# Three 1024-wide parts of an input projection (v, u, gate a) as seven half-size products each, in a hybrid decoder block on one Trainium2 core

## The chip, the cores and the metric

The kernel runs on 1 core of one Trainium2 chip. The metric is the device time of one execution in microseconds (us). An execution under the hardware profiler gives, beside its own time, a trace of every engine: TensorE (PE), VectorE (DVE), ScalarE (ACT), GpSimd (POOL), SyncE (SP), and of the transfers.

## The reference, cut to what matters

512 tokens of 1024 features go through one decoder block in fp32. The change touches only the first projection:

```python
h = rms_norm(x, g_mix)                       # x * rstd(token) * g_mix(feature)
z = h @ w_in                                 # [512, 1024] @ [1024, ...]
u, v, q_lat, kv_lat, k_rope, gate_a, gate_b = split(z)   # 1024, 1024, 384, 256, 64, 1024, 1024 wide
y_a = spatial_gating(gelu(u), gelu(v), ...)  # layer norm over v's 1024 columns, then a mix in chunks of 128 tokens
y_b = mla_attention(q_lat, kv_lat, k_rope, ...)
x = x + (sigmoid(gate_a) * y_a + sigmoid(gate_b) * y_b) @ w_o
# then a mixture of experts and a gated embedding: not touched
```

## The kernel before

Every fp32 matrix is split for TensorE into a high part (rounded to the type fp32r) and a low part (the rest). A product is three matmuls for each block of 128 features (a k-block): high rows by high weights, low rows by high weights, high rows by low weights. ScalarE makes the high part (a copy with rounding), VectorE the low part (the weights less their high part).

The projection runs in ten column chunks w = 0 to 9, in this order: q's latent (384 wide), the kv latent with the rope key (320 wide), v in two halves of 512, u in two, gate a in two, gate b in two. `z_chunk` does one chunk: 4 token tiles of 128 rows by 8 k-blocks by 3 matmuls, 96 in all (L1789, L1790, L1793), each token tile in one of four PSUM banks. SyncE's queue loads the weights of a chunk in one transfer (2048 KB for 512 columns) into one of the two buffers `win`; `split(w)` of ScalarE (L787) writes the high part times g_mix, `split(w)` of VectorE (L1222, one instruction with two inputs in SBUF for each k-block) the low part. The rows are x transposed, without g_mix. `evac` of ScalarE (L821 to L837) takes a finished bank out, for gate a in the bank itself, where VectorE multiplies it into u (L1299). `evac(1, t)` (L825, L826, L828) has three activations for one token tile: the kv latent, its sum of squares, that of the rope key. After chunk 9 attention goes on with transposes (L1743). GpSimd makes constants at the start, turns q by the rope tables (L627 to L629) and gathers rows for the experts later.

Each engine works through its own program in the order in which it is written; waits on semaphores stand in front of the instruction that needs them. So the order of the functions' calls for each engine decides what stands behind a wait.

## Time and profile before

| | us |
|---|---|
| runs | 1111.62, 1109.51, 1111.4 (median 1111.4) |
| the profiled execution's own time | 1110.49 |
| its span in the trace | 1108.7 |
| busy in the span: PE, PEld | 1092.9, 914.7 |
| busy in the span: DVE, ACT, POOL | 861.2, 787.0, 423.6 |

The span goes from the first to the last instruction in the trace; the execution's own time is 1.8 us more. PE is the matmuls, PEld the loads of the 128x128 operand that stays in the array, which run beside matmuls. Busy times of engines lie beside each other, so only the one that is waited for sets the end.

### The profile page before, as it was taken

What the parts mean: (1) busy time and instruction counts of PE and PEld (TensorE: products, weight loads), DVE (VectorE), ACT (ScalarE), POOL (GpSimd) and SP (SyncE); (2) the same over time, 40 slices, a digit from 0 to 9 for tenths busy, and PEclk for the clock granted to TensorE, in tenths of its full rate; (3) what the DMA queues carried; (4) which work ended last, traced back from release to release, by engine and by line L of the source; (5) the groups of instructions that cost most, each with busy time, mean ns of one, the idle gap of its engine ahead of it and who ended that gap; (6) DMA issues with size and microseconds to landing.
All of it is one profiled execution on the core that took longest, in us unless ns stands there. A gap on an engine that the chain in (4) does not pass through costs nothing.

```text
span 1108.7 us, 17836 instructions
## 1 busy us (share of the span) xinstructions
PE 1092.9 (99%) x5488; PEld 914.7 (83%) x5488; DVE 861.2 (78%) x1239; ACT 787.0 (71%) x1270; POOL 423.6 (38%) x477
## 2 busy tenths in 40 slices
PE   7999999999999999999999999999999999999998
PEld 7988888878778888888888888888888888888787
DVE  4535532278765468999999999999999999999865
ACT  6644433357654343888888898889888988888772
POOL 1120000015276003355556555555655555555400
PEclk9999999999999999999999999999999999999999
DMA  7422422112402259999999999999999999999632
GB/s 251 153 76 76 142 85 76 29 57 71 158 1 71 101 225 381 356 377 382 394 393 388 391 393 388 391 391 393 395 396 396 396 394 393 392 393 359 192 151 76
DMA packets 72130, 291.60 MB, mean 263 GB/s; under 512 B 15187, under 2 KB 20598, under 8 KB 47126
## 3 DMA queue, kind: packets, MB, share of 16 engines
q1 hardware_dynamic: 52672, 254.13, 57.3%
q0 software_dynamic: 18768, 34.79, 12.5%
q10 hardware_dynamic: 646, 2.12, 0.5%
q8 instruction: 24, 0.39, 0.1%
q14 instruction: 20, 0.16, 0.0%
HBM read 284.61 MB, written 42.07 MB: 295 GB/s over the span
## 4 chain that ended last, share of the span: by engine, by line
PE 93%; DVE 3%; ACT 2%; POOL 1%; issue 1%; DMA 0%; ACTq 0%; POOLq 0%; DVEq 0%
PE bank L2065 11%; PE bank L2067 11%; PE bank L2066 11%; PE bank L1752 7%; PE bank L1789 6%; PE bank L1793 6%; PE bank L1790 6%; PE bank L2093 5%; PE bank L2091 5%; PE bank L2092 5%; PE bank L2030 5%; PE bank L1743 2%; PE bank L1944 1%; PE bank L2163 1%; PE bank L2165 1%; PE bank L2164 1%
## 5 line engine op out<-in xcount | busy, mean ns | idle before, releaser
L1624 DVE TENSOR_TENSOR arena_r<-arena,win_r 128x1024 fp32r<-128x1024 f32 x252 | 292.0, 1221 | 21.9 <-ACT win_r L1082 19.1
L1082 ACT ACTIVATE win_r<-arena 128x1024 fp32r<-128x1024 f32 x252 | 246.5, 1069 | 0.5 <-DMA resid<-in_w_exp_up 0.5
L2065 PE MATMUL bank<-win_r,work_r 128*128 128x512 f32 x512 | 206.5, 403 | 0.6 <-issue 0.6
L2066 PE MATMUL bank<-win_r,x_low_r 128*128 128x512 f32 x512 | 199.5, 390 | 0.0
L2067 PE MATMUL bank<-arena_r,work_r 128*128 128x512 f32 x504 | 197.4, 392 | 0.0
L1604 DVE TENSOR_TENSOR arena_r<-arena,hT_r 128x1024 fp32r<-128x1024 f32 x128 | 150.5, 1217 | 0.5 <-ACT hT_r L1090 0.5
L733 POOL DMA_INDIRECT moe_sum<-ya,sidx x64 | 111.5, 1743 | 102.7 <-ACT ya L1118 86.0
L1789 PE MATMUL bank<-arena_r,hT_r 128*128 128x512 f32 (+2 forms) x320 | 121.9, 381 | 2.2 <-DVE win_r L1222 2.1
L1790 PE MATMUL bank<-arena_r 128*128 128x512 f32 (+2 forms) x320 | 121.1, 378 | 0.0
L1793 PE MATMUL bank<-win_r,hT_r 128*128 128x512 f32 (+2 forms) x320 | 121.0, 378 | 0.0
L2067 PEld LDWEIGHTS bank<-arena_r,work_r 128*128 128x128 f32 x504 | 94.6, 188 | 21.7
L2065 PEld LDWEIGHTS bank<-win_r,work_r 128*128 128x128 f32 x512 | 96.7, 189 | 18.8 <-issue 0.7
L2066 PEld LDWEIGHTS bank<-win_r,x_low_r 128*128 128x128 f32 x512 | 96.4, 188 | 18.6
L2091 PE MATMUL bank<-hT_r,work_r 128*128 128x512 f32 x256 | 105.2, 411 | 0.0
L708 POOL COPY small<-ya 128x1 f32 (+1 forms) x64 | 104.1, 1627 | 1.1 <-DMA ya<-h_rows,gidx 1.1
L2093 PE MATMUL bank<-arena_r,work_r 128*128 128x512 f32 x256 | 100.5, 393 | 0.0
L2092 PE MATMUL bank<-hT_r,work_r 128*128 128x512 f32 x256 | 100.0, 391 | 0.0
L1222 DVE SCALAR_TENSOR_TENSOR win_r<-win,small,arena_r 128x512 fp32r<-128x512 f32 (+2 forms) x80 | 54.2, 748 | 57.0 <-ACT arena_r L787 57.0
L693 POOL DMA_INDIRECT ya<-h_rows,gidx x66 | 69.7, 1055 | 53.1 <-POOL gidx L690 51.9
L627 POOL TENSOR_TENSOR work<-arena 128x256 f32<-128x256 f32 x10 | 7.7, 770 | 197.0 <-DVE arena L1378 180.9
L1589 DVE TENSOR_TENSOR x_low_r<-bank,work_r 128x512 fp32r<-128x512 f32 x128 | 82.0, 682 | 0.3 <-ACT work_r L1055 0.2
L1055 ACT ACTIVATE work_r<-bank 128x512 fp32r<-128x512 f32 x128 | 69.5, 595 | 13.3 <-PE bank L2030 11.5
(321 smaller groups left out, 2213.4 us busy)
## 6 DMA issues: line engine op xcount, KB each, us to landing
arena<-in_w_exp_down SPq DMA_DIRECT2D x64, 1024.0 KB
arena<-in_w_exp_gate SPq DMA_DIRECT2D x63, 1024.0 KB
arena<-in_w_exp_up SPq DMA_DIRECT2D x63, 1024.0 KB
win<-in_w_in SPq DMA_DIRECT2D x8, 2048.0 KB, 7.8
win<-in_w_o SPq DMA_DIRECT2D x2, 2048.0 KB, 7.9
arena<-in_w_ple_gate SPq DMA_DIRECT2D x2, 2048.0 KB, 13.7
arena<-moe_sum SPq DMA_DIRECT2D x7, 512.0 KB, 7.0
win<-in_mla_w_qb SPq DMA_DIRECT2D x4, 576.0 KB, 4.0
```

Of the source, the lines that this page charges most:

```text
L1082: act.activation(gu_hi[n % 2][:, :, cols], raw[:, :, cols], ACT.Copy).then_inc(gu_hi_r, 1)
L1604: dve.tensor_tensor(wdn_lo[j % RING][:, k, :], wdn[j % RING][:, k, :], wdn_hi[j % 2][:, k, :].bitcast(F32), ALU.subtract).then_inc(dn_lo, 1)
L1624: dve.tensor_tensor(low_[:, :, cols], raw[:, :, cols], gu_hi[n % 2][:, :, cols].bitcast(F32), ALU.subtract).then_inc(gu_lo_r, 1)
L1789: pe.matmul(b_, x_hi, w_hi, start=(k == 0), stop=False)
L1790: last = pe.matmul(b_, x_lo, w_hi, start=False, stop=False)
L1793: last = pe.matmul(b_, x_hi, w_lo, start=False, stop=(k == KD - 1))
L2065: pe.matmul(b_, x_hi[:, k, :], w_hi, start=(k == 0), stop=False)
L2066: pe.matmul(b_, x_lo[:, k, :], w_hi, start=False, stop=False)
L2067: last = pe.matmul(b_, x_hi[:, k, :], low_[:, :, k * FF:(k + 1) * FF], start=False, stop=(k == KD - 1))
L2091: pe.matmul(b_, hi, w_hi, start=(k == 0), stop=False)
L2092: pe.matmul(b_, lo, w_hi, start=False, stop=False)
L2093: last = pe.matmul(b_, hi, wdn_lo[n % RING][:, k, cols], start=False, stop=(k == KF - 1))
```

## The change

v, u and gate a (p = 0, 1, 2 in the new code) are cut in 2 x 2 blocks, tokens by columns, and their 1024 features in two halves. Eight products of half size become seven (Strassen's scheme in Winograd's form) at the price of sums ahead of and behind the products. They run in the order 11, T1, T2, 21, 22, T3, T4, each of 2 token tiles (i = 0, 1) by 4 k-blocks by 3 matmuls = 24 matmuls of 512 columns (L2243 to L2245), with banks by pairs. q's latent, the kv latent and gate b stay as they were.

- **Rows.** g_mix is now on the rows (when x is transposed: four activations of 128x128 for each half in `hT_evac`, L925; the low part multiplies by g_mix too, L1443). The weights are copied as they are, and VectorE's low part is a plain subtraction (L1547). Four sums of rows S1 to S4 (128x1024 each) are made by VectorE once (`rows_1` to `rows_4`, L1457 to L1479) and split like weights (`high_part`, `low_part`).
- **Weights.** Each half-size block has 128x2048 elements and is worked on in two parts of 128x1024. GpSimd makes the sums T1, T2 and T3 (`add_weights`, L749: for v T1, T2, T3; for u and for gate a T1, T3, T2), VectorE T4 (`last_weights`, L1504). ScalarE makes the high part of each block (L1009; L1002 for S), VectorE the low part (L1495; L1488 for S). They come in transfers of 1 MB where a chunk had one of 2 MB.
- **Outputs.** `add_products` (VectorE, L1520 to L1538) takes the products out of PSUM and adds them, two instructions of 128x512 for each of X, Y, 11, 12, 22, W, 21, each with one input in PSUM. "11" goes out first by ScalarE (`first_product_out`, L1014). `gelu` (L1022, L1024) works in SBUF.
- **Order.** evac(1, t) stands between the high parts of v in ScalarE's order; TensorE's product 11 of v waits for evac(1, i) to free its banks. v's layer-norm statistics for tokens 0 to 255 (`v_stats` 0 and 1) stand behind u's last sum, those for 256 to 511 between gate a's sums 12 and 22, and the split of chunk 8 (`FIRST`) between W and 21.
- **Buffers.** `resid` serves as a weight buffer, so x's rows are loaded again after T4 of gate a.

VectorE's order behind the low part of chunk 1. Before, that low part (L1222, 128x320) is followed by the rope angles and, behind them, the low parts of the 512-wide chunks:

```order
L1222 SCALAR_TENSOR_TENSOR win_r<-win,small,arena_r 128x320 x8
L1250 TENSOR_TENSOR work<-small,inv_freq 128x128
L1252 TENSOR_SCALAR work<-work 128x128
L1253 TENSOR_SCALAR work<-work 128x128
L1254 SCALAR_TENSOR_TENSOR work<-work 128x128
```

Now it is followed by the sums of rows and the low parts of v; `arena` holds S1, S2 and high parts, `work` S4, `rope_q` S3, `hT_r` is the high part of the rows, `resid`, `ya` and `win` hold weights (L1457 and L1458 are the two short pieces of one sum):

```order
L1463 TENSOR_TENSOR arena<-hT_r 128x1024
L1457 TENSOR_TENSOR arena<-arena,arena_r 128x512
L1458 TENSOR_TENSOR arena<-arena,arena_r 128x512
L1465 TENSOR_TENSOR arena<-arena,arena_r 128x1024
L1495 TENSOR_TENSOR arena_r<-resid,arena_r 128x1024 x2
L1495 TENSOR_TENSOR ya_r<-ya,arena_r 128x1024 x2
L1469 TENSOR_TENSOR arena<-arena,arena_r 128x1024
L1470 TENSOR_TENSOR arena<-arena,hT_r 128x1024
L1488 TENSOR_TENSOR arena_r<-arena,arena_r 128x1024
L1479 TENSOR_TENSOR work<-arena,hT_r 128x1024
L1457 TENSOR_TENSOR work<-work,arena_r 128x512
L1458 TENSOR_TENSOR work<-work,arena_r 128x512
```

The angles now stand behind v's last sum. GpSimd's order behind its constants, before (`gqr` is a gain, then the rope constants):

```order
L601 AFFINE_SELECT arena<-arena 128x1024
L605 TENSOR_SCALAR gqr<-gqr 128x64
L610 TENSOR_TENSOR arena<-work,gqr 128x128 x4
L610 TENSOR_TENSOR arena<-work,gkr 128x128 x4
L614 IOTA small 128x4
```

and now, where the 18 sums of weights stand in between (rows 2 to 4: T1, T2, T3 of v; then T1, T3, T2 of u and of gate a):

```order
L749 TENSOR_TENSOR resid<-ya 128x1024 x2
L749 TENSOR_TENSOR resid<-resid,win 128x1024 x2
L749 TENSOR_TENSOR ya<-ya,win 128x1024 x2
L749 TENSOR_TENSOR resid<-resid,win 128x1024 x2
L749 TENSOR_TENSOR win<-win 128x1024 x2
L749 TENSOR_TENSOR resid<-resid,win 128x1024 x4
L749 TENSOR_TENSOR win<-win 128x1024 x2
L749 TENSOR_TENSOR resid<-resid,win 128x1024 x2
L755 TENSOR_SCALAR gqr<-gqr 128x64
```

ScalarE's order at the start of v, now (`resid` is T1, `ya` block 11; L1002 are S1, S2 and S4; L986 to L989 are evac(1, t)). Before, this place had evac(1, 0) to evac(1, 3) with the next chunk's eight 128x512 copies of L787 between them:

```order
L1009 ACTIVATE arena_r<-resid 128x1024 x2
L1009 ACTIVATE arena_r<-ya 128x1024 x2
L1002 ACTIVATE arena_r<-arena 128x1024
L986 ACTIVATE arena<-bank,small 128x320
L987 ACTIVATE work,small<-bank,small 128x256
L989 ACTIVATE work,small<-bank,small 128x64
L1002 ACTIVATE arena_r<-arena 128x1024
L986 ACTIVATE arena<-bank,small 128x320
L987 ACTIVATE work,small<-bank,small 128x256
L989 ACTIVATE work,small<-bank,small 128x64
L1002 ACTIVATE work_r<-work 128x1024
L1009 ACTIVATE arena_r<-resid 128x1024 x2
```

So evac(1, 1), for which TensorE's product 11 waits with its second token tile, now stands behind S2's high part, and that behind VectorE's `rows_2`.

The diff, cut to its core:

```diff
+        NP = 3
+        in_res0, in_res1 = in_res
+        B_RAW = [{"11": in_ya[0], "T1": in_res0, "T2": in_res0, "21": in_w0[1], "22": in_w0[0], "T3": in_ya[1], "T4": in_res0}]
+        B_RAW += [{"11": in_w0[1], "T1": in_res[p % 2], "T2": in_res[p % 2], "21": in_w0[0], "22": in_w1[1], "T3": in_w1[0],
+                   "T4": in_res[p % 2]} for p in range(1, NP)]
+        B_HI = [{"11": in_v[0], "T1": in_v[1], "T2": in_hi[0], "21": in_tab, "22": in_ln, "T3": in_hi[0], "T4": in_hi[1]}]
+        B_HI += [{"11": in_hi[0], "T1": in_tab, "T2": in_hi[1], "21": in_tab, "22": in_ln, "T3": in_hi[0],
+                  "T4": in_tab if p == NP - 1 else in_hi[1]} for p in range(1, NP)]
+        B_LO = [{**B_RAW[0], "T1": in_ln, "T2": in_hi[1]}] + [{**B_RAW[p], "T1": in_ln, "T2": in_hi[0]} for p in range(1, NP)]
...
+        PRODUCTS = ("11", "T1", "T2", "21", "22", "T3", "T4")
+        PRODUCT_ROW = {"T1": "S1", "T2": "S2", "22": "S4", "T3": "S3"}
+        PRODUCT_BANK = {"11": 0, "T1": 4, "T2": 2, "21": 6, "22": 0, "T3": 4, "T4": 6}
+        HIGHS = [("T1", "11", "S1", "S2", "S4", "T2", "21", "22", "S3", "T3", "T4")] + [("T1", "11", "T2", "21", "22", "T3", "T4")] * (NP - 1)
+        LOWS = [("T1", "11", "S1", "S2", "T2", "S4", "21", "22", "S3", "T3", "T4")] + [("T1", "11", "T2", "21", "22", "T3", "T4")] * (NP - 1)
...
+        WEIGHTS_ORDER = [(0, n) for n in ("T1", "T2", "T3")] + [(p, n) for p in range(1, NP) for n in ("T1", "T3", "T2")]
...
+            def pairs_loads():
+                sp.wait_ge(tr_done, 2 * NT)
+                sp.wait_ge(rms_sq, NT)
+                half_load(v2(xr_, 2 * D, HK, 512), half_chunk(1, BASE[1]), ld_w0[0], 32)
+                free(0)
+                half_load(v2(win0, 0, HK, 512), half_chunk(0, "22"), win_ready[0], 32)
...
+                for p in range(2, NP):
+                    sp.wait_ge(pj_done, products_done(p - 2, "T4"))
+                    half_load(v2(xr_, p % 2 * 2 * D, HK, 512), half_chunk(p, BASE[p]), ld_w0[0], 16 + 16 * p)
+                    sp.wait_ge(pj_done, products_done(p - 1, "11"))
...
+            def add_weights(p, name):
+                done = 2 * WEIGHTS_ORDER.index((p, name))
+                if done:
+                    pool.wait_ge(weights_added, done)
+                term = "22" if name != "T1" else "11" if BASE[p] == "12" else "12"
+                pool.wait_ge(*raw_landed(p, term))
+                if name == "T1" and p == 0:
+                    pool.wait_ge(*raw_landed(0, "11"))
+                    pool.wait_ge(tr_done, 2 * NT)
+                    pool.wait_ge(rms_sq, NT)
+                elif name == "T1":
+                    pool.wait_ge(ld_w0[0], 16 + 16 * p)
+                elif name == "T3":
+                    pool.wait_ge(*raw_landed(p, "12"))
+                else:
+                    pool.wait_ge(lo_ready, split_count(LOWS, p, "T1"))
+                for part in range(2):
+                    dst, other = B_RAW[p][name][part][0], (B_RAW[p]["T3"] if term == "12" else B_RAW[p][term])[part][0]
+                    src = B_RAW[0]["11"][part][0] if name == "T1" and p == 0 else dst
+                    pool.tensor_tensor(dst, src, other, ALU.add).then_inc(weights_added, 1)
+            for p, name in WEIGHTS_ORDER:
+                add_weights(p, name)
...
-                    act.activation(whi_r[:, k, 0:n], v2(win[w % 2], 0, KD, n)[:, k, :], ACT.Copy,
-                                   scale=gmix[:, k:k + 1]).then_inc(hi_ready, 1)
+                    if w == FIRST:
+                        act.wait_ge(pj_done, products_done(NP - 1, "T3" if k < HK else "T2"))
+                    elif w >= 1:
+                        act.wait_ge(whi_used, KD * (w - 1 if w == 1 else w - 1 - 2 * NP) + k + 2)
+                    z = slice(k, k + step)
+                    act.activation(whi_r[:, z, 0:n], v2(win[w % 2], 0, KD, n)[:, z, :], ACT.Copy).then_inc(hi_ready, step)
...
+            high_part(0, "T1")
+            high_part(0, "11")
+            high_part(0, "S1")
+            evac(1, 0)
+            high_part(0, "S2")
+            evac(1, 1)
+            high_part(0, "S4")
+            act.wait_ge(whi_used, 2 * KD)
+            high_part(0, "T2")
+            evac(1, 2)
+            evac(1, 3)
+            high_part(0, "21")
+            first_product_out(0)
+            high_part(0, "22", products_done(0, "T1"))
+            high_part(0, "S3")
+            high_part(0, "T3", products_done(0, "T2"))
+            high_part(0, "T4", products_done(0, "T2"))
+            for p in range(NP):
+                gelu(p, "11")
+                if p + 1 < NP:
+                    high_part(p + 1, "T1", products_done(p, "21"))
+                gelu(p, "12")
+                if p + 1 < NP:
+                    high_part(p + 1, "11", products_done(p, "T3"))
+                else:
+                    split(FIRST, range(HK))
+                    split(FIRST, range(HK, KD))
+                gelu(p, "22")
+                gelu(p, "21")
+                if p + 1 < NP:
+                    first_product_out(p + 1)
+                    high_part(p + 1, "T2", products_done(p, "T4"))
+                    high_part(p + 1, "21", products_done(p + 1, "T1"))
+                    high_part(p + 1, "22", products_done(p + 1, "T1"))
+                    high_part(p + 1, "T3", products_done(p + 1, "T2"))
+                    high_part(p + 1, "T4", products_done(p + 1, "21" if p + 1 == NP - 1 else "T2"))
...
-                    dve.scalar_tensor_tensor(v2(win_r[w % 2], 0, KD, n)[:, k, :], v2(win[w % 2], 0, KD, n)[:, k, :],
-                                             gmix[:, k:k + 1], whi_r[:, k, 0:n].bitcast(F32), ALU.mult, ALU.subtract).then_inc(lo_ready, 1)
...
+            def rows_1():
+                for i in range(2):
+                    dve.wait_ge(tr_free[i], NT)
+                link(dve.tensor_tensor(S1, row_hi(lower, second), row_hi(upper, second), ALU.subtract))
+                link(lower_lo(S1, second, ALU.add))
+                dve.tensor_tensor(S1, S1, row_lo(0, second), ALU.subtract).then_inc(combined, 1)
...
+            def rows_2():
+                dve.wait_ge(combined, 1)
+                link(dve.tensor_tensor(S2, S1, row_lo(0, first), ALU.add))
+                dve.tensor_tensor(S2, S2, row_hi(upper, first), ALU.add).then_inc(combined, 1)
...
+            def low_part(p, name, room=None):
+                if room is not None:
+                    dve.wait_ge(pj_done, room)
+                if name[0] == "S":
+                    dve.wait_ge(hi_ready, split_count(HIGHS, p, name))
+                    dve.tensor_tensor(s_lo[name], s_raw[name], s_hi[name].bitcast(F32), ALU.subtract).then_inc(lo_ready, 1)
+                    return
+                for part in range(2):
+                    dve.wait_ge(hi_ready, split_count(HIGHS, p, name, part))
+                    reader = {"11": "T1", "21": "T4", "22": "T2" if p else "T3"}.get(name)
+                    if reader is not None:
+                        dve.wait_ge(*added(p, reader, part))
+                    dve.tensor_tensor(B_LO[p][name][part][1], B_RAW[p][name][part][0], B_HI[p][name][part][1].bitcast(F32),
+                                      ALU.subtract).then_inc(lo_ready, 1)
+            def last_weights(p):
+                dve.wait_ge(*raw_landed(p, "21"))
+                dve.wait_ge(lo_ready, split_count(LOWS, p, "T2"))
+                for part in range(2):
+                    dst = B_RAW[p]["T4"][part][0]
+                    dve.tensor_tensor(dst, dst, B_RAW[p]["21"][part][0], ALU.add).then_inc(combined, 1)
...
+                product = {"X": "T2", "Y": "T1", "11": "21", "12": "22", "22": "T3", "W": "T3", "21": "T4"}[quad]
...
+                        dve.tensor_tensor(C21, b_, C12, ALU.subtract).then_inc(pj_free[2 + i], 2)
...
+            rows_1()
+            low_part(0, "T1")
+            low_part(0, "11")
+            rows_2()
+            low_part(0, "S1")
+            rows_4()
+            low_part(0, "S2")
+            low_part(0, "T2")
+            last_weights(0)
+            low_part(0, "S4")
+            low_part(0, "21")
+            low_part(0, "22")
+            rows_3()
+            low_part(0, "S3")
...
+            for p in range(NP):
+                add_products(p, "X")
+                add_products(p, "Y")
+                low_part(p, "T3")
+                low_part(p, "T4")
+                add_products(p, "11")
+                if p == 2:
+                    gated_quad("11")
+                if p + 1 < NP:
+                    low_part(p + 1, "T1", products_done(p, "22"))
+                add_products(p, "12")
+                if p == 2:
+                    gated_quad("12")
+                    v_stats(2)
+                    v_stats(3)
+                add_products(p, "22")
+                add_products(p, "W")
+                if p + 1 < NP:
+                    low_part(p + 1, "11")
+                else:
+                    split(FIRST, range(HK))
+                    split(FIRST, range(HK, KD))
+                add_products(p, "21")
+                if p == 0:
+                    means_and_angles()
+                elif p == 1 and NP == 3:
+                    v_stats(0)
+                    v_stats(1)
+                if p + 1 < NP:
+                    low_part(p + 1, "T2", products_done(p + 1, "11"))
+                    last_weights(p + 1)
+                    low_part(p + 1, "21")
+                    low_part(p + 1, "22")
...
+                    for k in range(HK):
+                        if i == 0 and k % 2 == 0:
+                            pe.wait_ge(lo_ready, split_count(LOWS, p, name, k // 2))
+                        if row is not None:
+                            a_hi, a_lo = s_hi[row][:, k, tok(i)], s_lo[row][:, k, tok(i)]
+                        else:
+                            k_, q = (k if name == "11" else k + HK), tok(i + 2 if name == "T4" else i)
+                            a_hi, a_lo = hT_hi[:, k_, q], lo_[k_][:, q]
+                        w_hi, w_lo = B_HI[p][name][k // 2][1][:, k % 2, :], B_LO[p][name][k // 2][1][:, k % 2, :]
+                        b_ = bank[b0 + i][:, :]
+                        pe.matmul(b_, a_hi, w_hi, start=(k == 0), stop=False)
+                        pe.matmul(b_, a_lo, w_hi, start=False, stop=False)
+                        last = pe.matmul(b_, a_hi, w_lo, start=False, stop=(k == HK - 1))
+                last.then_inc(pj_done, 2 if name == "T4" else 1)
```

## Rows read from the trace of the kernel before

**Rows 1.** The page: engines' busy time, and slices of PE and its clock

```profile
PE 1092.9 (99%) x5488; PEld 914.7 (83%) x5488; DVE 861.2 (78%) x1239; ACT 787.0 (71%) x1270; POOL 423.6 (38%) x477
...
PE   7999999999999999999999999999999999999998
...
PEclk9999999999999999999999999999999999999999
```

**Rows 2.** Windows, v and u: PE, PEld, DVE, ACT, POOL busy; clock, DMA share, GB/s

```profile
47.50:134.50 87.00, 87.00 (x386) 72.03 (x385) 45.43 (x67) 40.86 (x62) 5.79 (x6) 1.00 0.27 95
```

**Rows 3.** Timeline of ScalarE, gate a: start, duration, instruction, idle before and its releaser

```profile
159.40 0.66 ACT L835 ACTIVATE bank<-bank,small 128x512 f32<-128x512 f32 x1 [4.40 <-PE bank L1793]
164.84 0.66 ACT L835 ACTIVATE bank<-bank,small 128x512 f32<-128x512 f32 x1 [4.78 <-PE bank L1793]
170.28 0.66 ACT L835 ACTIVATE bank<-bank,small 128x512 f32<-128x512 f32 x1 [4.78 <-PE bank L1793]
```

**Rows 4.** Timeline of TensorE: v's first matmuls, and pauses at 8 and 288

```profile
8.36 0.66 PE L1789 MATMUL bank<-arena_r,hT_r 128*128 128x384 f32 x1 [2.10 <-DVE win_r L1222]
...
12.72 0.45 PE L1790 MATMUL bank<-arena_r 128*128 128x384 f32 x1
...
44.96 0.39 PE L1790 MATMUL bank<-arena_r 128*128 128x512 f32 x1
...
288.71 0.98 PE L1743 MATMUL bank<-ident,arena 128*128 128x128 f32 x7 [1.20 <-DVE arena L1378]
```

**Rows 5.** Groups by line and shape: busy, mean ns of one, idle before

```profile
L1624 DVE TENSOR_TENSOR arena_r<-arena,win_r 128x1024 fp32r<-128x1024 f32 x252 | 292.0, 1221 | 21.9 <-ACT win_r L1082 19.1 <-issue 0.9
L1082 ACT ACTIVATE win_r<-arena 128x1024 fp32r<-128x1024 f32 x252 | 246.5, 1069 | 0.5 <-DMA resid<-in_w_exp_up 0.5
L1589 DVE TENSOR_TENSOR x_low_r<-bank,work_r 128x512 fp32r<-128x512 f32 x128 | 82.0, 682 | 0.3 <-ACT work_r L1055 0.2
L676 POOL TENSOR_TENSOR arena_r<-arena,hT_r 128x1024 fp32r<-128x1024 f32 x2 | 4.8, 2401 | 0.8 <-DVE tops L1528 0.8
```

**Rows 6.** Timeline of VectorE: chunk 1's low parts, then long instructions in pairs

```profile
28.86 3.32 DVE L1222 SCALAR_TENSOR_TENSOR win_r<-win,small,arena_r 128x320 fp32r<-128x320 f32 x7
...
502.39 2.36 DVE L1624 TENSOR_TENSOR arena_r<-arena,win_r 128x1024 fp32r<-128x1024 f32 x2
...
507.33 1.28 DVE L1589 TENSOR_TENSOR x_low_r<-bank,work_r 128x512 fp32r<-128x512 f32 x2
```

**Rows 7.** Timeline, low parts of chunk 3 beside GpSimd's turn of q

```profile
63.76 2.38 DVE L1222 SCALAR_TENSOR_TENSOR win_r<-win,small,arena_r 128x512 fp32r<-128x512 f32 x2
64.92 2.37 DVE L1222 SCALAR_TENSOR_TENSOR win_r<-win,small,arena_r 128x512 fp32r<-128x512 f32 x2
...
68.35 1.40 DVE L1222 SCALAR_TENSOR_TENSOR win_r<-win,small,arena_r 128x512 fp32r<-128x512 f32 x2
...
64.52 1.07 POOL L627 TENSOR_TENSOR work<-arena 128x256 f32<-128x256 f32 x1
...
247.67 0.73 POOL L629 TENSOR_TENSOR work<-work 128x256 f32<-128x256 f32 x1
```

**Rows 8.** Timeline, a long low part beside GpSimd, and the same kind alone

```profile
215.57 1.36 DVE L1305 TENSOR_TENSOR win_r<-win,win_r 128x1152 fp32r<-128x1152 f32 x1 [16.81 <-ACT win_r L845]
...
243.09 1.57 DVE L1305 TENSOR_TENSOR win_r<-win,win_r 128x1152 fp32r<-128x1152 f32 x1 [0.47 <-ACT win_r L845]
...
243.41 1.85 POOL L628 TENSOR_TENSOR work<-arena 128x256 f32<-128x256 f32 x1
```

**Rows 9.** Transfers: KB each, median us from issue to landing

```profile
win<-in_w_in SPq DMA_DIRECT2D x8, 2048.0 KB, 7.8
...
win<-in_mla_w_qb SPq DMA_DIRECT2D x4, 576.0 KB, 4.0
```

417 lines of the change are left out of this document (316 added, 101 removed).

## The prediction, on record before the kernel ran

> **What bounds the kernel now.** First the page [rows 1]: TensorE is busy 1092.9 of 1108.7 us, VectorE 861.2, ScalarE 787.0, and the row of PE by slices shows nines from the second slice to the last but one. So nothing but TensorE's own work sets the end. Then the windows [rows 2]: from 47.5 to 134.5, most of v and u, TensorE works 87.00 of 87.00 us at a granted clock of 1.00, VectorE 45.43, ScalarE 40.86, GpSimd 5.79. The reader is to see two things. Matmuls taken out here come off the time one for one. And they come off only while the other engines, now about half busy, keep up: VectorE has 41.6 us free in these 87. Last the timelines of one engine, for what one instruction takes. I work in the span's time (1108.7; the execution's own time was 1110.49, and the median of the runs, 1111.4, stands 0.9 above that), and add the 0.9 at the end.
>
> **What is removed.** ScalarE takes out a bank of gate a at 159.40, 164.84 and 170.28 [rows 3]: 24 matmuls in 5.44 us, 0.227 each. v, u and gate a were 6 chunks x 4 = 24 such groups, and are 21 now. 3 x 5.44 = **16.3 us less**. That is all that the change can gain.
>
> **What is added on TensorE's path at the start.** g_mix on the rows makes four small activations of one, ahead of the first products. TensorE starts those at 8.36 with a pause of 2.10 before it [rows 4], so it waits for others there. I put the start at 0.3 later: v began at 44.73, one matmul ahead of the row at 44.96 [rows 4], and begins at 45.0 now. Bounds 0 and 1.
>
> **What is added on VectorE, and when it is due.** TensorE's product 11 of u needs VectorE's low part of block 11 of u. v is seven products of 5.44 = 38.1 us, so this is due at 45.0 + 38.1 = 83.1. The order of the program lets VectorE begin with `rows_1` when the low part of chunk 1 is done: at 32.2 before [rows 6], some 33.1 now, with the later start and GpSimd beside it. From there to the first half of that low part stand
> - 31 instructions of 128x1024 with both inputs in SBUF: sums of rows 8 (2, 2, 1, 3), low parts of S 4, low parts of blocks 14 of v and 3 of u, T4's sums 2. The nearest row is the same operation on the same shape in the experts: mean 1.221 [rows 5], and two in a row take 2.36, so 1.14 from start to start [rows 6]. 31 x 1.14 = 35.3.
> - 4 of 128x512 (the short pieces of two sums of rows), at 0.61, worked out as half of 1.22: 2.4.
> - 12 of 128x512 with one input in PSUM (X, Y, 11, 12, 22, W of v): mean 0.682 [rows 5], two in a row 1.28, so 0.60: 7.2.
> - 8 places where an instruction must wait until the one ahead of it is done, 0.12 each (an estimate: 1.22 alone against 1.14 in a row, and a little more): 1.0.
>
> That is 45.9. When I lay ScalarE's program (copies of 128x1024 at 1.069 [rows 5], evac and gelu between them) beside it, VectorE also waits for ScalarE three times: 0.8 before T2, 1.1 before S3, 1.7 before u's T1, whose high part stands behind a gelu. In all 33.1 + 45.9 + 3.6 = 82.6: **0.5 us to spare**, if GpSimd costs nothing. This is the thin place of the change: VectorE goes from half busy to nearly full in front of a TensorE that has got faster.
>
> **What GpSimd's sums cost.** 18 instructions of 128x1024, 2.40 each undisturbed [rows 5]; 8 of them (T2 and T3 of v, T1 and T3 of u) are free to run between about 39 and 65, beside VectorE's two-input instructions. Is that free? The rows say no. While GpSimd turns q with 128x256 instructions, VectorE's low parts of 128x512 start at 63.76 and 64.92, 1.16 apart; when GpSimd has ended, two take 1.40 together [rows 7]. GpSimd's instruction in that place takes 1.07 instead of 0.73 [rows 7]. And a GpSimd instruction of that size that starts 0.32 after a long low part of VectorE takes 1.85, and ends 0.6 after it; the low part takes 1.57 instead of 1.36 [rows 8]. Both read as if the two took turns, one whole instruction at a time: with a GpSimd instruction of 256 columns in each turn VectorE loses 1.16 - 0.68 = 0.48. For 1024 columns the turn is longer by 2.40 - 0.74: VectorE loses 0.48 + 1.66 = 2.14 for each. The lower bound is nothing, the upper one 2.40 (the whole instruction).
>
> The Trainium skill, page "SBUF — State Buffer", section "Who interferes with whom", says why: VectorE and GpSimd share one pair of ports, an exclusive lock held for a whole instruction, and a VectorE instruction with two SBUF inputs needs it against a GpSimd instruction that reads SBUF, one with at most one SBUF input doesn't. The trace agrees [rows 7, 8]. By the page's whole-instruction lock alone each sum would cost VectorE its 2.40, 8 x 2.40 = 19.2 in place of 17.1. The page lets the one that issues first block the other; who gets the next turn it does not say.
>
> 8 x 2.14 = 17.1, less the 0.5 to spare: u starts **16.6 us late**. It need not come as one wait. Laid out in order, TensorE waits about 4.5 in the middle of v's 11 (evac(1, 1) is behind S2's high part, and `rows_2` runs into the first sums), 6 before T2, 2 before T3 and 3.6 before u's 11. Gate a's T1 (2 sums) falls beside u's low parts of 21 and 22: of its 4.3, TensorE's product 21 of u sees about **1.4**. u's T2 and gate a's T3 and T2, 6 sums, lie beside `add_products` with an input in PSUM, or where VectorE waits anyway: nothing; if that is wrong, up to 6 x 2.14 = 12.8 less the slack of a pair (38.1 against some 33 of VectorE's work), so up to about 8.
>
> **What I cost at nothing.** The transfers: 2048 KB landed in 7.8 and 576 in 4.0 [rows 9], so 1 MB in about 5.1, and each is issued when a product of the pair before has freed its buffer, over 10 us ahead; 95 GB/s moved here [rows 2]. v_stats and the split of chunk 8 inside gate a: behind gate a's last low parts no TensorE product of the pair waits for them, and by my layout VectorE is at chunk 8's low parts just as gate a's last product ends (under 0.1 of a wait); without that cover up to 2. The second load of x: used some 100 us later. `first_product_out` and the linked waits of `add_products` on ScalarE: 0.
>
> **The sum.** -16.3 (matmuls) + 16.6 (u late) + 1.4 (gate a's T1) + 0.3 (start) = +2.0. 1110.5 + 2.0 = 1112.5, with the 0.9 a median of 1113.4; as I have laid the turns without a gap, which they will have here and there, I say **1113**. A measurement of this kernel tells about 0.2%, 2.2 us, from no change: 1109.2 to 1113.6 is "same".
>
> **The rivals.**
> - A, forecast, turns taken one by one, 0.45: 1113. Its own range is 1109 to 1117, by the turn (1.9 to 2.4: 8 x 0.25 = 2 each way) and 2 for the start and gate a.
> - B, VectorE goes first, 0.22. GpSimd gets in only where VectorE waits or works from PSUM. Then VectorE loses only where it waits for a sum that it needs: T2 and T3 of v in two parts each, 4 x 2.40 = 9.6, less the 0.8 of ScalarE's wait that falls together with them and the 0.5 to spare: u 8.3 late. -16.3 + 8.3 + 0.3 = -7.7: 1103 to 1104. For it: VectorE goes on back to back [rows 7] while GpSimd stretches too. Against it: a VectorE that goes first would not have gone from 0.68 to 1.16.
> - C, everything is hidden, 0.08. -16.3 + 0.3 + 0 to 1: 1095 to 1096. It needs fp32 adds of GpSimd that cost VectorE nothing; [rows 7] speak against it.
> - D, on the slower side, 0.20: the clock. TensorE's first products after its pause of 2.10 at 8.36 run at half pace: from the row at 8.36 to the row at 12.72 [rows 4] there are 13 matmuls of 384 columns in 4.36, 1.15 columns per ns, the lower level (1.2 GHz), against 13 x 0.17 = 2.2 at the rate of [rows 3], the upper one (2.4 GHz): 2.1 lost. The page's row of the clock stands at 9 in these slices all the same [rows 1], so it is the pitch that has to be looked at. After the only long pause later on, 1.20 us before 288.71 [rows 4], nothing is slower: seven transposes take 0.98 together. No row shows what a pause of 3.6 to 6 us in the middle does. If it costs the same 2.1, the pauses inside v hide it behind VectorE, and the one before u's 11 does not: 1115; with one in u or gate a as well, 1117. It decides from a single pause of 3 or more that has no later wait of v behind it.
> - The rest, 0.05: a transfer that is late, or much more loss in u and gate a, 1118 to 1125.
>
> The Trainium skill, page "TensorE: Matmul & The Clock Gate", has the array at the lower of two levels, 1.2 and 2.4 GHz, when it has been idle, and at the upper one when busy; the two paces of the trace agree with it [rows 3, 4], and by it D would come true. No row of this case shows which pause brings the lower one back.
>
> **How the numbers follow.** The time is A's, 1113. The range takes A, D and B: 1101 to 1118; below it C, above it the rest, with bits of the others some 2 in 10. Faster by over 0.2% (under 1109.2): B, C and a little of A, 0.33. Same: most of A and a bit of B, 0.29. Slower (over 1113.6): D, the rest, and A's upper part, 0.38.
>
> **What would show it.** In the profile after: 72 matmuls of 512 columns fewer, TensorE's busy time down by about 16 and its idle time up by about as much. v's first product at about 45.3, u's first at about 100 instead of 83 (B: 91; C: 83 to 84); gate b's first matmul near 177, where with nothing lost it would be at 45.0 + 21 x 5.44 = 159. GpSimd's sums at 3.2 us instead of 2.4 where they lie beside VectorE's 128x1024 instructions, and VectorE's starts there 3.3 apart instead of 1.14. TensorE's first pause in 11 of v, released by ScalarE's evac. Beside sums with an input in PSUM, GpSimd's at 2.4 and VectorE's at 0.60 to 0.68. After each pause the pitch of the matmuls: 0.227, or twice that (D). What would make it wrong: turns that are not one for one, a spare time of VectorE that is not 0.5 but 5 (then 1109) or less than nothing, and a price in u and gate a that I put at 1.4.

## The result: slower, above the range

The changed kernel takes 1119.53 us (median of 4 runs, 1118.29 to 1119.93), the kernel before 1111.14 beside it (4 runs): ratio 1.0076, 95% interval 1.0059 to 1.0094. The prediction was 1113 with a range to 1118. The span went from 1108.7 to 1117.9, so 9.2 us are to be found in the two traces.

The page of the changed kernel, the rows that answer to [rows 1]:

```profile
PE 1087.2 (97%) x5416; PEld 907.6 (81%) x5416; DVE 947.9 (85%) x1305; ACT 801.3 (72%) x1285; POOL 485.2 (43%) x495
...
PE   7888999999999999999999999999999999999998
...
PEclk9988999999999999999999999999999999999999
```

72 matmuls are gone (5488 to 5416), 16.3 us of work, but TensorE is busy only 5.7 us less. The row of the clock shows most of the reason: eights in the third and fourth slice, where it was nine throughout. Busy time at half pace is still busy time. By the starts of the products below, half pace takes 8.7 of the missing 10.6 us; the rest was not taken apart. And the row of PE shows eights in slices 2 to 4, where it stands idle.

Windows of the changed kernel: v's first wait, what follows it, the rest of v, the first five products of u, then the last ones of u with gate a (columns: PE, PEld, DVE, ACT, POOL busy, granted clock, DMA share, GB/s):

```profile
45.00:53.00 8.00, 3.85 (x20) 3.01 (x18) 7.97 (x3) 2.08 (x6) 7.92 (x3) 0.94 0.73 252
53.00:64.00 11.00, 10.80 (x36) 8.62 (x36) 10.93 (x5) 1.04 (x3) 10.84 (x5) 0.73 0.02 8
64.00:97.50 33.50, 29.57 (x122) 23.51 (x120) 30.37 (x31) 20.26 (x32) 3.50 (x2) 0.95 0.19 63
97.50:137.00 39.50, 33.98 (x131) 27.35 (x131) 33.35 (x47) 18.08 (x22) 8.77 (x4) 0.87 0.26 82
137.00:184.00 47.00, 47.00 (x208) 38.54 (x206) 40.09 (x56) 26.15 (x31) 10.74 (x5) 1.00 0.32 111
```

Where [rows 2] had TensorE at 87.00 of 87.00, VectorE and GpSimd are now both full from 45 to 64 (7.97 and 7.92 of 8, 10.93 and 10.84 of 11) and TensorE waits. Two engines that are busy all the time with 3 and 3, then 5 and 5 instructions are not working side by side: they take turns. The last window, the end of u and gate a, runs at 47.00 of 47.00 at full clock: there the change costs nothing.

VectorE and GpSimd of the changed kernel, timeline of that stretch:

```profile
44.15 3.42 DVE L1469 TENSOR_TENSOR arena<-arena,arena_r 128x1024 f32<-128x1024 f32 x1
47.60 3.28 DVE L1470 TENSOR_TENSOR arena<-arena,hT_r 128x1024 f32<-128x1024 f32 x1
50.81 3.36 DVE L1488 TENSOR_TENSOR arena_r<-arena,arena_r 128x1024 fp32r<-128x1024 f32 x1
...
57.52 2.75 DVE L1457 TENSOR_TENSOR work<-work,arena_r 128x512 f32<-128x512 f32 x1
...
66.32 2.35 DVE L1495 TENSOR_TENSOR arena_r<-resid,arena_r 128x1024 fp32r<-128x1024 f32 x2
...
98.64 2.47 DVE L1495 TENSOR_TENSOR win_r<-win,arena_r 128x1024 fp32r<-128x1024 f32 x1
...
39.91 6.58 POOL L749 TENSOR_TENSOR resid<-resid,win 128x1024 f32<-128x1024 f32 x2 [9.51 <-DVE arena_r L1495]
46.56 6.53 POOL L749 TENSOR_TENSOR ya<-ya,win 128x1024 f32<-128x1024 f32 x2
...
95.30 4.72 POOL L749 TENSOR_TENSOR resid<-resid,win 128x1024 f32<-128x1024 f32 x2 [30.00 <-DVE arena_r L1495]
```

VectorE's instructions start 3.3 us apart, GpSimd's pairs take 6.55, 3.28 each: the same number, one for one. Alone they take 1.14 and 2.40 [rows 5, 6]. Even a VectorE instruction of 512 columns takes 2.75, so it loses a whole turn as well. The low part of v's T2 starts at 66.32, when GpSimd's eight sums are done, and takes its plain time. GpSimd's pair at 95.30 (T2 of u), beside sums from PSUM, takes its plain 4.72, but its end falls beside the low part of u's 11 at 98.64, which takes 2.47.

TensorE of the changed kernel, the four pauses (in brackets the idle time ahead and its releaser) and what follows two of them:

```profile
53.20 0.80 PE L2243 MATMUL bank<-arena_r,hT_r 128*128 128x512 f32 x1 [4.35 <-ACT work L989]
53.79 0.63 PE L2244 MATMUL bank<-arena_r 128*128 128x512 f32 x1
54.22 0.63 PE L2245 MATMUL bank<-ya_r,hT_r 128*128 128x512 f32 x1
...
67.67 0.47 PE L2243 MATMUL bank<-arena_r 128*128 128x512 f32 x1 [3.33 <-DVE arena_r L1495]
...
101.25 0.77 PE L2243 MATMUL bank<-arena_r,hT_r 128*128 128x512 f32 x1 [3.62 <-DVE win_r L1495]
...
122.28 0.47 PE L2243 MATMUL bank<-arena_r,hT_r 128*128 128x512 f32 x1 [1.89 <-DVE win_r L1495]
...
124.13 0.63 PE L2244 MATMUL bank<-arena_r 128*128 128x512 f32 x1
124.56 0.63 PE L2245 MATMUL bank<-win_r,hT_r 128*128 128x512 f32 x1
```

After each of them the matmuls of 512 columns start 0.43 apart for a while (53.79 to 54.22, 124.13 to 124.56), where 0.227 is the full pace. 512 columns in 0.43 us are 1.2 per ns, the lower level of 1.2 GHz. After the first pause and the one before u's 11 this begins at once, after the other two some 1.5 us later, and it takes 7 to 12 matmuls. The stretches cost 2.60 and 1.73 us in v's 11 and T2. From here the 9.2 us can be put together from starts of products. v starts at 45.94, 1.2 later than before. u starts at 101.25, 17.2 later than v's seven products need. Of u, 11 takes 8.10 and 21 takes 7.19 where 5.44 is the norm, 2.66 and 1.75 more, and before 21 there are 2.05 of pause. Some 0.65 come before chunk 8. 1.2 + 17.2 + 2.66 + 1.75 + 2.05 + 0.65 - 16.3 = 9.2.

### The profile page after: what moved, and what is told of

Same layout as the page of the kernel before. It is cut to its first block, busy times and chain, and to the rows that moved or that the text cites. A ratio compares the mean times of both kernels' runs of the same rounds, so it can differ in the third digit from the quotient of the medians.

```text
span 1117.9 us, 17853 instructions
## 1 busy us (share of the span) xinstructions
PE 1087.2 (97%) x5416; PEld 907.6 (81%) x5416; DVE 947.9 (85%) x1305; ACT 801.3 (72%) x1285; POOL 485.2 (43%) x495
## 4 chain that ended last, share of the span: by engine, by line
PE 83%; DVE 10%; ACT 3%; issue 2%; POOL 1%; DMA 0%; DVEq 0%; ACTq 0%
PE bank L2517 11%; PE bank L2519 11%; PE bank L2518 10%; PE bank L2151 7%; PE bank L2545 5%; PE bank L2544 5%; PE bank L2543 5%; PE bank L2482 5%; PE bank L2142 2%; PE bank L2187 2%; PE bank L2191 2%; PE bank L2188 2%; PE bank L2243 1%; PE bank L2244 1%; PE bank L2245 1%
## 5 line engine op out<-in xcount | busy, mean ns | idle before, releaser
L883 POOL DMA_INDIRECT moe_sum<-ya,sidx x64 | 117.7, 1839 | 98.1 <-ACT ya L1346 75.7
L2545 PE MATMUL bank<-arena_r,work_r 128*128 128x512 f32 x256 | 100.5, 393 | 0.0
L875 POOL COPY sidx<-slot_tokens 128x1 uint32 (+1 forms) x64 | 78.1, 1221 | 2.3 <-DMA moe_sum<-ya,sidx 2.3
L1343 ACT ACTIVATE ya<-bank 128x512 f32<-128x512 f32 x64 | 38.4, 601 | 48.5 <-PE bank L2545 48.5
L2151 PE MATMUL bank<-win_r,arena_r 128*128 128x512 f32 (+1 forms) x224 | 72.6, 373 | 0.3 <-DVE win_r L1702 0.3
L840 POOL COPY gidx<-slot_tokens 128x1 uint32 (+1 forms) x66 | 15.3, 232 | 125.9 <-PE bank L2482 117.0
L1318 ACT ACTIVATE hT_r<-arena 128x1024 fp32r<-128x1024 f32 x65 | 69.0, 1063 | 0.0
```

Source lines behind the costliest of these rows:

```text
L883: pool.indirect_dma_start(sums[j % 2], bass.IndirectOffsetOnAxis(sidx[j % 2][0:NS, 0:1], 0), yo[j % 2][0:NS], None, bounds_check=last_toke ...
L2151: last = pe.matmul(bank[b_][:, 0:width], l, r, start=(i == 0), stop=(i == len(pairs) - 1))
L2545: last = pe.matmul(b_, hi, wdn_lo[n % RING][:, k, cols], start=False, stop=(k == KF - 1))
```

## The experiments

The runs were made in three sets, each with the kernel before beside it (medians 1110.5, 1110.6 and 1110.7, and 1111.1 beside the changed kernel). A difference of medians from two sets is uncertain by some 0.6 us for that alone.

**The sums taken out.** Only the size of GpSimd's instructions is changed; nearly all of the sums is left out.

```diff
-                    pool.tensor_tensor(dst, src, other, ALU.add).then_inc(weights_added, 1)
+                    pool.tensor_tensor(dst[:, :, 0:2], src[:, :, 0:2], other[:, :, 0:2], ALU.add).then_inc(weights_added, 1)
```

> GpSimd's 18 sums of weights work on 4 of 1024 columns in each instruction, so nearly all of the sums is left out and GpSimd needs the shared turn for next to nothing; every semaphore and every other instruction stays. Theory (GpSimd's whole instructions take turns with VectorE's, and the pauses that follow also drop TensorE's clock): VectorE's long instructions keep 1.14 us from start to start, u starts within 1 us of the end of v's seven products, no half-pace stretch, and the time falls by 16.3 less the later start of v (1.2) less about 0.6 before chunk 8: 1096 to 1098. Rival (VectorE's added work alone is too much, and GpSimd beside it is only a symptom): u stays over 8 us late and the time stays above 1108.

Measured: 1095.38 us (4 runs), ratio to the kernel before 0.9867 (0.985 to 0.9883), span 1093.8. VectorE and TensorE of this kernel:

```profile
43.95 1.21 DVE L1488 TENSOR_TENSOR arena_r<-arena,arena_r 128x1024 fp32r<-128x1024 f32 x1
45.09 1.21 DVE L1479 TENSOR_TENSOR work<-arena,hT_r 128x1024 f32<-128x1024 f32 x1
46.34 0.69 DVE L1457 TENSOR_TENSOR work<-work,arena_r 128x512 f32<-128x512 f32 x1
47.06 0.69 DVE L1458 TENSOR_TENSOR work<-work,arena_r 128x512 f32<-128x512 f32 x1
47.67 1.22 DVE L1488 TENSOR_TENSOR arena_r<-arena,arena_r 128x1024 fp32r<-128x1024 f32 x1
49.83 1.23 DVE L1495 TENSOR_TENSOR arena_r<-resid,arena_r 128x1024 fp32r<-128x1024 f32 x1 [0.94 <-ACT arena_r L1009]
...
83.29 0.39 PE L2245 MATMUL bank<-resid_r,hT_r 128*128 128x512 f32 x1
83.54 0.47 PE L2243 MATMUL bank<-arena_r,hT_r 128*128 128x512 f32 x1
```

u's 11 follows v's T4 without a pause (83.29, 83.54), and TensorE runs at full pace through all 21 products. The time is 0.6 below the forecast: v started at 45.41, 0.7 later than before and not 1.2, and 0.3 came before chunk 8 in place of 0.6. So the whole loss of 24 us of the changed kernel against this one (1119.53 - 1095.38) hangs on the size of GpSimd's 18 instructions, 15.1 us below the kernel before (1110.5 beside it) is what the change would bring without them, and VectorE's own added work fits, with nothing to spare: T2's low part, which started at 66.32 in the changed kernel, starts at 49.83 here, 16.5 earlier.

**The early sums on VectorE.** T2 and T3 of v and T1 and T3 of u are the same instruction on the other engine.

```diff
+        DVE_ORDER = [(0, 'T2'), (0, 'T3'), (1, 'T1'), (1, 'T3')]
...
             low_part(0, "11")
+            dve_weights(0, "T2")
...
+                    dve.tensor_tensor(dst, dst, other, ALU.add).then_inc(dve_added, 1)
```

> The four early sums that lie beside VectorE's long instructions (T2 and T3 of v, T1 and T3 of u, 8 instructions of 128x1024) are made by VectorE itself instead of by GpSimd; the other ten stay with GpSimd. Theory (a GpSimd sum costs VectorE a turn of 2.14 us there, its own one 1.14 at the spacing in a row): u starts 8 us earlier than in the changed kernel, near 93, with a shorter pause and, if the pause is what drops the clock, perhaps less half pace in u: 1107 to 1112. Rival (GpSimd's sums cost VectorE less than the row says, so that more work on VectorE is a loss): u at 101 or later, 1119 or more.

Measured: 1110.76 us (10 runs), ratio 1.0005 (0.9995 to 1.0014). u starts at 94.21, 7.0 earlier (8 were forecast). Eight sums on the engine that is short of time, and it is faster by 8.8 us than with them on the idle one. The span is shorter by 9.0. 7.0 are u's start, and 2.55 the half pace that did not come in u's 11 (5.55 us where it took 8.10): behind a pause of 3.2 us it runs at 0.227. The pause of 2.05 before u's 21 is there as before, and so is half pace behind it.

```profile
94.22 0.47 PE L2270 MATMUL bank<-arena_r,hT_r 128*128 128x512 f32 x1 [3.04 <-DVE win_r L1503]
94.52 0.39 PE L2271 MATMUL bank<-arena_r 128*128 128x512 f32 x1
94.75 0.40 PE L2272 MATMUL bank<-win_r,hT_r 128*128 128x512 f32 x1
```

**ScalarE's order in v.**

```diff
-            high_part(0, "S2")
             evac(1, 1)
+            high_part(0, "S2")
             high_part(0, "S4")
```

> In ScalarE's program evac(1, 1) stands ahead of S2's high part instead of behind it; nothing else changes. Theory (everything in v before u's 11 is hidden behind VectorE's chain): the pause of 4.5 us in the middle of v's 11 is gone, and as much or more comes back before T1 and T2 of v; u starts at 101 as before, and the time stays within 1 us of 1119.5. Rival (that first pause and the half pace behind it are on the path): 3 to 5 us less, 1114.5 to 1116.5.

Measured: 1118.88 us (4 runs), ratio 1.0077 (1.0061 to 1.0094). TensorE of this kernel, its pauses in v:

```profile
54.25 0.50 PE L2243 MATMUL bank<-arena_r 128*128 128x512 f32 x1 [2.70 <-DVE arena_r L1488]
...
67.67 0.77 PE L2243 MATMUL bank<-arena_r 128*128 128x512 f32 x1 [6.07 <-DVE arena_r L1495]
```

The pause in 11 is gone, and comes back before T1 and as a pause of 6.07 before T2, which starts at 67.67 as in the changed kernel; u starts at 101.26. So the pause in v's 11 and the half pace behind it are not on the path, as the theory said. The first wait that one sees in a trace is not what sets the end here; VectorE's chain is.

**Unread matmuls in the waits, v and u.** They write banks that the next product starts anew.

```diff
+            WARM = {'bank4': 18, (0, 'T2', 0): 14, (1, '11', 0): 15, (1, '21', 0): 8}
...
+                    for _ in range(WARM.get((p, name, i), 0)):
+                        pe.matmul(bank[b0 + i][:, :], hT_hi[:, 0, tok(i)], hT_hi[:, 0, :], start=True, stop=True)
```

> The changed kernel with matmuls that nobody reads in front of four waits of TensorE (18 in the middle of v's 11, 14 before T2 of v, 15 before u's 11, 8 before u's 21), so that TensorE does not stand idle there; everything else stays. Theory (the pause before u's 11 drops the clock, and the half pace in u's 11 puts off ScalarE's and VectorE's next steps, which brings the pause before 21 and a second half-pace stretch): u and its 21 run at 0.227 throughout, u's seven products take 38 to 39 us where they took 44.5, and the time falls by 5 to 6.5, to 1113 to 1114.5. u itself starts as late as before, near 101. Rival (the half pace is hidden behind VectorE as inside v): within 1.5 us of 1119.5.

Measured: 1117.5 us (4 runs), ratio 1.0064 (1.0048 to 1.0081): 2.0 less than the changed kernel, where 5 to 6.5 were forecast, by a fault of the edit: the 14 before T2 stood behind the wait for ScalarE's evac, so they came late, ran at half pace themselves (5.99 us for 14) and put T2 off to 73.2, v ended at 100.5, and the 15 before u's 11 held it until 103.86. u then took 40.2 us instead of 44.5, without half pace. It left the question of u's share open, hence the next.

**Unread matmuls in u alone.**

```diff
+            WARM = {(1, '11', 0): 15, (1, '21', 0): 8}
```

> The changed kernel with unread matmuls in front of u only: 15 (3.4 us) ahead of the wait of u's 11, where TensorE stood for 3.78, and 8 (1.8 us) ahead of that of u's 21, where it stood for 2.05. Nothing in v. Theory (half pace behind these two pauses is on the path: 2.6 us in u's 11, 1.75 in 21): u starts at 101.3 as in the changed kernel, every product of u runs at 0.227, the pause before 21 stays, since GpSimd's sum for gate a moves forward with TensorE, and the time falls by 4.3, to 1114.5 to 1116. Rival (only what comes behind 21 counts, as in the run with matmuls in v too, where the gain was 2.0): 1117 to 1118.

Measured: 1115.11 us (6 runs), ratio 1.0034 (1.0022 to 1.0046), 4.4 less than the changed kernel. Its TensorE around u's start, the 15 matmuls in one row:

```profile
97.12 3.56 PE L2243 MATMUL bank<-hT_r 128*128 128x512 f32 x15
100.86 0.50 PE L2256 MATMUL bank<-arena_r,hT_r 128*128 128x512 f32 x1 [0.18 <-DVE win_r L1495]
101.20 0.39 PE L2257 MATMUL bank<-arena_r 128*128 128x512 f32 x1
101.43 0.39 PE L2258 MATMUL bank<-win_r,hT_r 128*128 128x512 f32 x1
```

0.23 apart at once, where the changed kernel had 0.43. More work on TensorE, less time. By the traces, chunk 8 starts 4.60 earlier (179.92 against 184.52): u's 11 takes 2.52 less and its 21 1.62 less, 4.1 in all for the half pace, where 2.66 + 1.75 = 4.4 was counted; 0.4 more is u's start at 100.86, which comes from a start of v 0.6 earlier and not from the edit. So the agreement of 4.4 with 4.4 is luck by 0.3.

**Gate a's T1 later.**

```diff
+                if (p, name) == (2, 'T1'):
+                    pool.wait_ge(pj_free[2], 6)
```

> GpSimd's T1 of gate a waits until VectorE has done the first X of u, instead of starting as soon as its block lands, beside T4's sum and the low parts of 21 and 22 of u. Nothing else changes. Theory (those two sums cost VectorE 4.3 us of turns there, which TensorE's 21 of u sees as a pause of 2.05 and a half-pace stretch of 1.75): the pause before u's 21 and its half pace are gone, and the time falls by 3.8, to 1115 to 1116.5. Rival (the pause has another cause, ScalarE's high parts behind u's slow 11): still there, within 1 us of 1119.5.

Measured: 1114.7 us (10 runs, 1113.03 to 1118.07), ratio 1.0035 (1.0023 to 1.0046), 0.3 below the forecast. In the traces chunk 8 starts 3.8 earlier, as forecast. VectorE and GpSimd of this kernel:

```profile
114.21 2.36 DVE L1506 TENSOR_TENSOR resid<-resid,win 128x1024 f32<-128x1024 f32 x2
116.49 4.62 DVE L1497 TENSOR_TENSOR win_r<-win,arena_r 128x1024 fp32r<-128x1024 f32 x4
...
123.42 5.25 DVE L1497 TENSOR_TENSOR win_r<-win,arena_r 128x1024 fp32r<-128x1024 f32 x2
...
121.84 5.74 POOL L751 TENSOR_TENSOR resid<-resid,win 128x1024 f32<-128x1024 f32 x2 [21.89 <-DVE ya L1522]
```

T4's sum and the four low parts take their plain times, and the pause before u's 21 is gone with its half pace. The turns were not avoided, only moved: T3's low parts take 5.25 instead of 2.36 now, where TensorE does not come for them until later.

**GpSimd's instructions cut in half.**

```diff
-                    pool.tensor_tensor(dst, src, other, ALU.add).then_inc(weights_added, 1)
+                    pool.tensor_tensor(dst[:, 0:1, :], src[:, 0:1, :], other[:, 0:1, :], ALU.add)
+                    pool.tensor_tensor(dst[:, 1:2, :], src[:, 1:2, :], other[:, 1:2, :], ALU.add).then_inc(weights_added, 1)
```

> The changed kernel with each of GpSimd's 18 sums of 128x1024 cut into two of 128x512, all else the same. Theory (the two engines take turns instruction by instruction, so a shorter GpSimd instruction costs less per turn, but there are twice as many turns; by the rows of the kernel before 16 x 1.0 = 16 us in place of 8 x 2.14 = 17): VectorE's long instructions start 2.2 us apart instead of 3.3 for twice as many of them, u starts 0 to 2 us earlier, 1117 to 1120. Rival (the turn costs VectorE a fixed amount whatever GpSimd's size): VectorE loses twice as much, u 10 us or more later still, over 1125.

Measured: 1115.62 us (4 runs), ratio 1.0046 (1.0031 to 1.0062): 1.4 below the range that the theory gave, and nowhere near the rival. VectorE and GpSimd of this kernel:

```profile
44.95 2.20 DVE L1471 TENSOR_TENSOR arena<-arena,hT_r 128x1024 f32<-128x1024 f32 x1
47.07 2.31 DVE L1489 TENSOR_TENSOR arena_r<-arena,arena_r 128x1024 fp32r<-128x1024 f32 x1
49.31 2.30 DVE L1480 TENSOR_TENSOR work<-arena,hT_r 128x1024 f32<-128x1024 f32 x1
...
43.79 2.28 POOL L749 TENSOR_TENSOR resid<-resid,win 128x512 f32<-128x512 f32 x1
46.03 2.28 POOL L750 TENSOR_TENSOR resid<-resid,win 128x512 f32<-128x512 f32 x1
```

The turns are 2.24 now, again one for one. u starts at 99.67, 1.6 earlier. Another 2.4 by chunk 8 come in u and gate a: u's 11 takes 7.40 instead of 8.10, the pause of 2.05 before 21 is gone, and 21 takes 6.20 instead of 7.19; a pause of 1.25 in gate a's T1 is new. Why the pause before 21 is gone I did not follow up.

**The sums placed by what VectorE does.** T2, T3 of v and T3 of u on VectorE, GpSimd's others moved (waits as in the expectation), and the same with unread matmuls ahead of u's 11:

```diff
+        DVE_ORDER = [(0, 'T2'), (0, 'T3'), (1, 'T3')]
...
+                if (p, name) == (1, 'T1'):
+                    pool.wait_ge(combined, COMBINED.index((0, "S3", 0)) + 1)
+                if (p, name) == (1, 'T2'):
+                    pool.wait_ge(lo_ready, split_count(LOWS, 1, "11"))
+                if (p, name) == (2, 'T1'):
+                    pool.wait_ge(pj_free[2], 6)
```

> The same sums, placed by what VectorE does: VectorE makes T2 and T3 of v and T3 of u itself (the last behind the angles, where it waits); GpSimd makes T1 of u from the end of S3's sum on (beside a wait and sums from PSUM), T2 of u once the low part of 11 of u is done, T1 of gate a from the first X of u on. Theory: counted from the run without sums (1095.4): start 0.5 later, two sums on VectorE 4.6 less a wait of 0.9, T1 of u 1.3, and half pace behind the pause before u's 11 2.5, so u starts near 90 and the time is 1102 to 1105. Rival (turns are lost wherever GpSimd works, PSUM or not): u's 11 and 21 each 2 us or more later still, 1107 to 1110.

> The kernel with the sums placed by what VectorE does, and 20 unread matmuls (4.5 us) ahead of the wait of u's 11. Theory (the pause there drops the clock, and u's 11 behind it is on the path): u's 11 at 0.227 throughout and 2 to 2.6 less than without them: 1100 to 1102.5. If the pause is shorter than 4.5, the matmuls themselves hold u up by the difference. Rival (the half pace is hidden by VectorE's work for u): the same as without them within 0.7.

Measured: 1107.33 us (6 runs), ratio 0.9968 (0.9956 to 0.998), and with the matmuls 1107.8 (7 runs), 0.9969 (0.9958 to 0.998). Both forecasts missed: the first by 2.3 above its upper end, which puts the time into the rival's range, the second by 5.3. But u's 11 started at 89.40 as the theory said, and not 2 us later as the rival did. The pause before it was only 0.9, with no half pace behind, so there was none for the 4.5 us of unread matmuls of the second kernel to save. The times are the same within 0.7, as the rival of the second says, but not because half pace was hidden. The matmuls held u's 11 up to 93.12, and that cost little in the end (chunk 8 starts at 172.12 instead of 171.37): the new pause of 2.96 before u's T2, with half pace, that the first kernel has, is gone there, u's 21 starts at 109.44 instead of 110.49, and pauses of 0.70 and 1.77 in gate a took back what was won. VectorE of the first kernel shows where the pause before T2 is from:

```profile
91.51 1.46 DVE L1437 TENSOR_SCALAR small<-small 128x4 f32<-128x4 f32 x1
...
92.95 2.37 DVE L1437 TENSOR_SCALAR small<-small 128x4 f32<-128x4 f32 x1
...
90.52 4.76 POOL L763 TENSOR_TENSOR resid<-resid,win 128x1024 f32<-128x1024 f32 x2 [16.05 <-DVE win_r L1509]
```

I had put GpSimd's T2 of u beside the small instructions of the angles, as harmless. A VectorE instruction on 4 columns with one input waits for the whole of GpSimd's: 1.46 and 2.37. The three take 3.81 together, where they take 0.30 with no GpSimd instruction beside them. Behind the angles VectorE's own T3 of u (2.28) stands ahead of T2's low part as well, so the pause has two sources.

**Second arrangement.** T2 of u back beside the sums from PSUM, T3 of u behind T2's low part, gate a's T2 and T3 behind the low part of its 11.

```diff
+        WEIGHTS_ORDER = [z for z in ([(0, n) for n in ("T1", "T2", "T3")] + [(p, n) for p in range(1, NP) for n in ("T1", "T2", "T3")]) if z not in DVE_ORDER]
...
+                if (p, name) == (2, "T2"):
+                    pool.wait_ge(lo_ready, split_count(LOWS, 2, "11"))
...
+                    if p == 0:
+                        dve_weights(1, "T3")
```

> The kernel with the sums placed by what VectorE does, in a second arrangement: T2 of u by GpSimd as soon as T1's low part is done (beside sums from PSUM) and not beside the small instructions of the angles; T3 of u by VectorE behind the low part of T2, not ahead of it; gate a's T2 and T3 by GpSimd behind the low part of gate a's 11. Theory (turns are lost beside any VectorE instruction that needs the shared turn, tensor_scalar on 128x4 too, which took 1.46 and 2.37 us there): u's 11 starts about 1.2 us later (90.6), the pause before T2 of u (2.96) and its half pace (1.7) are gone, 3 us less than in the first arrangement: 1103 to 1105.5. Rival (what the first arrangement lost behind u's 11 was not GpSimd's turn, but VectorE's T3 ahead of T2's low part alone): 1 to 2 us less, 1105.5 to 1106.5.

Measured: 1106.56 us (5 runs), ratio 0.9964 (0.995 to 0.9977). The pause before T2 of u and its half pace are gone, and u's 11 starts at 91.05, as forecast within 0.5; but a pause of 1.3 came before gate a's 11, and 0.5 in its T2, which I had not counted, so the gain was 0.8 and not 3 (the medians' own scatter is about 1). The time lies 1.1 above the theory's range and 0.1 above the rival's (1105.5 to 1106.5). The angles took their plain 0.29 here, so GpSimd's turn was part of the loss, but both T2 of u and T3 of u were moved in one edit, and how the pause of 2.96 divides between them is not shown. It is the fastest of the versions that make all the sums: 4 us below the kernel before, 13 under the changed one, and 11 above the one without sums.

## Why the prediction failed, step by step

**What bounds the kernel, what is removed.** Held: 16.3 us less of matmuls, and they count only while VectorE keeps up (15.1 less without GpSimd's sums, 8.4 more with them).

**VectorE's chain, 0.5 us to spare.** Held. Without GpSimd's sums it went from 33.14 to 83.4, 50.2 long where the forecast has 49.5, and TensorE came for it at 83.5. Its three waits for ScalarE were 0.94, 1.13 and 1.83, forecast as 0.8, 1.1 and 1.7. Some 0.1 was to spare.

**GpSimd's sums, 2.14 each in turns.** Held, place (39.91 to 65.31) and size. T2's low part starts at 66.32 against 49.83 without sums, 16.5 later, of which 0.4 was there when `rows_1` began: the eight early sums put VectorE off by 16.1. As they covered its wait of 0.94 before T2, they cost 17.0; forecast 17.1. u 17.2 late, forecast 16.6. That this is so near is in part luck, as two misses cancel: the forecast did not take off the wait that the sums cover (0.9), and it put at nothing that T2 of u ran partly beside u's low part of 11 (2.47 instead of 1.22, 1.25 more). The forecast's waits of TensorE inside v were 4.5, 6 and 2 where the trace has 4.51, 3.48 and 0.75: there half pace (4.3 us) filled what would have been waiting, as rival D says. Rival B, VectorE goes first, is excluded by the spacing of 3.3 for both engines, rival C by the run without sums: 1095.4 was its time, but it takes leaving the sums out.

**Gate a's T1, 1.4.** Too small: the pause is 2.05, and with the half pace behind it 3.8; the run with gate a's T1 later shows it, 3.8 at chunk 8 and 4.0 in the span.

**The start, 0.3, bounds 0 and 1.** Too small: v starts at 45.94, 1.2 later. In the ten other kernels with the same start it lies between 45.28 and 45.99, so 0.6 to 1.3 later. The four small activations for each half take 1.14 together where one took 0.60, 1.1 in all for the two halves; that they are what delays v no run shows by itself, nor why it varies.

**The step that failed is the clock at nothing in the sum.** The prediction priced half pace only in rival D, 2.1 for a stretch, with a chance of 0.20, and made the forecast without it. Its grounds were that nothing was slower behind a pause of 1.20 and that no row showed what a longer one in the middle does. The trace shows half pace behind all four pauses, two of the stretches on the path: 2.66 in u's 11 and 1.75 in 21. Filling the two waits with unread matmuls gave 4.1 of these 4.4 back, which shows that they were on the path. So D was right in mechanism and near in size (1117 with two such stretches, 4.2 in all), and it belonged into the forecast: the forecast's own laid-out order had pauses of 4.5, 6, 2 and 3.6 us in TensorE, and the only row of a pause over 2 us [rows 4] was followed by half pace. D alone would still have been 2.5 too low. From the forecast's +2.0 to the 9.2 of the traces it is 4.4 for the clock, 0.9 for the start, 0.6 for u, 0.65 for the pause before 21 (2.05 in place of 1.4) and 0.65 before chunk 8, which was put at under 0.1.

What stays open: which pause is followed by half pace. 4.51, 3.48, 3.78 and 2.05 us were in the changed kernel; 3.20 in the kernel with sums on VectorE and 2.23 in the last one were not. The clearest case is the pause of 3.48 before v's T2: the kernel with gate a's T1 later has it too, behind the same work, and runs at full pace (69.50 to 69.73) where the changed kernel was at half pace from 69.1 to 72.5:

```profile
67.60 0.47 PE L2245 MATMUL bank<-arena_r 128*128 128x512 f32 x1 [3.32 <-DVE arena_r L1497]
...
69.50 0.39 PE L2247 MATMUL bank<-arena_r 128*128 128x512 f32 x1
69.73 0.39 PE L2245 MATMUL bank<-arena_r 128*128 128x512 f32 x1
```

So neither the length of the pause nor the work before it decides it. The executions of that one kernel differ as well: over the whole span the granted clock was 0.992 in the two slowest of its ten (1116.20 and 1118.07 us) and 0.993 to 0.995 in the others (1113.03 to 1115.68).
